# Gate and modulation chunks re-placed beside the second block's attention units, and a barrier crossed with scan work, in a two-block fp32 network kernel

## The reference, cut to what matters

```python
h_l = modulate(xl, norm_mix_g[l], mod_l[0], mod_l[1])        # mod = silu(c) @ ada_w[l] + ada_b[l]
ql, kl, vl, zl, xbcl, dtfl, dtbl, gal, gsl = in_proj_split(h_l @ w_in)
s = jnp.einsum('bqhcd,bkhcd->bchqk', q, k) * (ATT_HEAD_DIM ** -0.5)   # 8 heads, two maps each
p = jax.nn.softmax(s, axis=-1)
a = p[:, 0] - lam * p[:, 1]
o = jnp.einsum('bhqk,bkhe->bqhe', a, v)
att = rmsnorm(o, subln_g) * (1.0 - lam_init)
dt_f = jax.nn.softplus(dtf_raw + dt_bias_f)                  # the scan's time steps, 64 columns of h @ w_in
ssd = ssd_output(...)                                        # conv, two-way chunked scan, norm
merge = (sigmoid(ga) * (att @ w_attn_o) + sigmoid(gs) * ssd) @ w_out
```

## Time and profile before

| | |
|---|---|
| three runs, median (lowest to highest) | 2977.1 us (2976.78 to 2983.97) |
| the profiled execution, its own time | 2984.38 us |
| its span, first to last instruction | 2982.6 us |
| PE busy | 2920.2 us (98%) |
| PEld busy | 2391.0 us (80%) |
| DVE busy | 1452.4 us (49%) |
| ACT busy | 814.4 us (27%) |
| POOL busy | 1019.8 us (34%) |
| mean granted TensorE clock | 0.995 |

### The profile page before, as it was taken

One profiled execution on the slowest core, in us unless ns is written; L12 is line 12 of the kernel. 1 busy time (PEld: TensorE's weight loads), 2 busy tenths in 40 slices (PEclk: granted clock), 3 DMA queues, 4 the chain that ended last, 5 costly groups with the idle time before them and its releaser, 6 DMA issues.

```text
span 2982.6 us, 40515 instructions
## 1 busy us (share of the span) xinstructions
PE 2920.2 (98%) x16088; PEld 2391.0 (80%) x16088; DVE 1452.4 (49%) x2765; ACT 814.4 (27%) x1778; POOL 1019.8 (34%) x876
## 2 busy tenths in 40 slices
PE   8999999999999999999999999999999999999999
PEld 7777899998855558888888888888876766678998
DVE  1243377713265638787753442343247555541651
ACT  1022222201033326766610220111013355540210
POOL 0000333674500125565643244443330112210786
PEclk9999999999999899999999999999999999999999
DMA  7456344442255133222232122222330332234443
GB/s 261 146 208 254 127 156 166 159 170 85 99 212 212 43 128 114 101 112 96 89 129 87 71 96 85 85 85 85 113 113 29 128 113 103 102 121 148 149 170 114
DMA packets 68977, 377.63 MB, mean 127 GB/s; under 512 B 6378, under 2 KB 24874, under 8 KB 26304
## 3 DMA queue, kind: packets, MB, share of 16 engines
q1 hardware_dynamic: 49120, 334.60, 30.9%
q10 hardware_dynamic: 18704, 36.90, 3.7%
q0 software_dynamic: 976, 3.63, 0.3%
HBM read 366.50 MB, written 4.42 MB: 124 GB/s over the span
## 4 chain that ended last, share of the span: by engine, by line
PE 61%; DVE 7%; ACT 2%; PEld 1%; issue 1%; POOL 0%; PEldq 0%; POOLq 0%; ACTq 0%; DVEq 0%
PE PB L501 12%; PE PB L629 9%; PE PA L501 7%; PE PB L1513 6%; PE PS L501 6%; PE PB L381 5%; PE PB L1187 2%; PE PB L1486 2%; PE PB L425 2%; PE PA L1573 1%; PE PA L1609 1%; PE PA L1592 1%; DVE work L2905 1%; ACT work L1984 1%; PE PB L1527 1%; DVE small L2704 1%
## 5 line engine op out<-in xcount | busy, mean ns | idle before, releaser
L536 POOL TENSOR_TENSOR sums<-ring 128x512 f32<-128x512 f32 x115 | 151.2, 1315 | 603.3 <-PE PA L501 246.9
L501 PE MATMUL PB<-work,sums 128*128 128x128 f32 (+1 forms) x1360 | 230.6, 327 | 0.0
L1513 PE MATMUL PB<-H,ring 128*128 128x512 f32 (+1 forms) x576 | 228.3, 545 | 0.0
L501 PEld LDWEIGHTS PB<-work,sums 128*128 128x128 f32 x1360 | 207.1, 191 | 17.5
L501 PE MATMUL PA<-work,sums 128*128 128x128 f32 (+1 forms) x1280 | 208.9, 318 | 0.0
L734 DVE TENSOR_TENSOR work<-PA,work 128x128 f32<-128x128 f32 (+1 forms) x53 | 18.9, 356 | 379.8 <-ACT work L718 379.8
L501 PEld LDWEIGHTS PA<-work,sums 128*128 128x128 f32 x1280 | 187.5, 191 | 13.5
L3204 POOL TENSOR_TENSOR work<-work 128x256 f32<-128x256 f32 x96 | 59.7, 642 | 386.3 <-ACT work L2072 327.1
L1513 PEld LDWEIGHTS PB<-H,ring 128*128 128x128 f32 x576 | 108.7, 191 | 95.7 <-issue 91.4
L734 DVE TENSOR_TENSOR work<-PB,work 128x256 f32<-128x256 f32 (+1 forms) x34 | 13.0, 381 | 320.9 <-ACT work L718 320.9
L541 POOL TENSOR_TENSOR sums<-ring,sums 128x512 f32<-128x512 f32 x115 | 151.6, 1318 | 9.0
(11 more groups left out here) (441 smaller groups left out, 6144.1 us busy)
## 6 DMA issues: line engine op xcount, KB each, us to landing
ring<-stream SPq DMA_DIRECT2D x314, 1024.0 KB, 4.8
sums<-cs_rows ACTq DMA_DIRECT2D x16, 1024.0 KB, 4.6
sums<-cs_rows ACTq DMA_DIRECT2D x16, 512.0 KB, 3.9
work<-work ACTq DMA_DIRECT2D x16, 256.0 KB, 4.4
work<-scratch POOLq DMA_DIRECT2D x1, 2560.0 KB, 13.5
mrg_kept<-work ACTq DMA_DIRECT2D x1, 2048.0 KB, 10.7
work<-mrg_kept ACTq DMA_DIRECT2D x1, 2048.0 KB, 9.7
X<-xT SPq DMA_DIRECT2D x2, 512.0 KB, 5.7
```

The costliest lines, as they stand in the source:

```text
L501: mm = pe.matmul(fast_bank(side, bank)[:, col:col + width], weight(k), right(4 * part + k), start=first and opens and k == 0, stop=last an ...
L536: nc.gpsimd.tensor_tensor(su[:, 0], a21, a22, ALU.add).then_inc(sem("w_summed"), 1)
L1513: mm = pe.matmul(PB[:, pair, t, 0:Tc], ring[:, c % SLOTS, k, t * P:(t + 1) * P], H[:, k, 0:Tc], start=(k == 0), stop=(k == KT - 1))
```

## The change

Four things, with no work added or removed. First, the gate chunks 1 to 3 of layer 0 move from units 12, 20, 28 to 8, 20, 31, and the 24 modulation chunks from units 1 to 24 to units 1 to 30 without 5, 8, 9, 14, 20 and 21. Second, in layer 1 the gate chunks, which stood whole beside units 1, 6 and 11, go by halves: units 1 and 4, 7 and 10, 13 and 16. Third, the last gate chunk's second half is split into four rows of weights each and put into the tail behind the last scores (steps 31 to 33, and 16 and 17 in layer 1). DVE and ACT copy out that last chunk behind their loops. Fourth, at the barrier PE does `project(0, (0,))` between its count and its wait; the time-step product is cut in two, of which one half stands behind the wait and the other behind head 0's sum and `project(0, (1,))`.

```diff
+ADA_BESIDE = [u for u in range(1, 31) if u not in (5, 8, 9, 14, 20, 21)]
+GA_PIECES = [
+    {8: ([(1, 0, 0, KT)], [(1, 1, 0, KT)]), 20: ([(2, 0, 0, KT)], [(2, 1, 0, KT)]), 31: ([(3, 0, 0, KT)], []),
+     32: ([], [(3, 1, 0, 4)]), 33: ([], [(3, 1, 4, KT)])},
+    {1: ([(1, 0, 0, KT)], []), 4: ([(1, 1, 0, KT)], []), 7: ([(2, 0, 0, KT)], []), 10: ([(2, 1, 0, KT)], []),
+     13: ([(3, 0, 0, KT)], []), 16: ([], [(3, 1, 0, 4)]), 17: ([], [(3, 1, 4, KT)])}]
...
-    units, gated = (32, (12, 20, 28)) if la == 0 else (16, (1, 6, 11))
+    units, gated = (32, (8, 20, 31)) if la == 0 else (16, (4, 10, 15))
...
-            + ([(f"ada{la + 1}", u - 1)] if la == 0 and 1 <= u <= ADA_CHUNKS else []) for u in range(units)]
+            + ([(f"ada{la + 1}", ADA_BESIDE.index(u))] if la == 0 and u in ADA_BESIDE else []) for u in range(units)]
...
             eng.drain().then_inc(stage_end, 1)
+            if meanwhile:
+                meanwhile()
             eng.wait_ge(stage_end, 4 * barriers[who])
...
                     if u < len(us):
                         scores2(u)
-                        beside(attention_fill(la)[u], T, 0)
+                        beside(modulation, T, 0)
+                    for piece in ahead:
+                        ga_piece(*piece)
                     if 2 <= u <= len(us) + 1:
                         turn2(u - 2)
-                    if u < len(us):
-                        beside(attention_fill(la)[u], T, 1)
+                    for piece in behind:
+                        ga_piece(*piece)
+                    beside(modulation, T, 1)
                     if u >= 3:
                         values2(u - 3)
                 held.finish(ada_second)
-                bar()
...
+                pe.wait_ge(sem("w_exp"), LAYER["w_exp"] * la + 2 * len(us))
+                bar(lambda: project(0, (0,)))
+                dt_product((0, 1))
                 for h in range(8):
...
-                    project(0, (h,))
+                    project(0, (h + 1,) if h < 7 else ())
+                    if h == 0:
+                        dt_product((2, 3)).then_inc(sem("dt_sum"), 1)
```

More of the change, by code:

```diff
@@ L80 @@
 HALF_AT = [i for i in range(A_UNITS) if i % 8 not in (2, 7)]
+ADA_BESIDE = [u for u in range(1, 31) if u not in (5, 8, 9, 14, 20, 21)]
[4 more added lines that the diff above has]
+     13: ([(3, 0, 0, KT)], []), 16: ([], [(3, 1, 0, 4)]), 17: ([], [(3, 1, 4, KT)])}]
+assert len(ADA_BESIDE) == ADA_CHUNKS
 assert 3 * len(ADA_AT) == ADA_CHUNKS and len(HALF_AT) == 2 * 3 * D // CHUNK
@@ L309, in program, with barrier @@
         barriers = {}
-        def barrier(eng, who):
+        def barrier(eng, who, meanwhile=None):
             barriers[who] = barriers.get(who, 0) + 1
             eng.drain().then_inc(stage_end, 1)
+            if meanwhile:
+                meanwhile()
             eng.wait_ge(stage_end, 4 * barriers[who])
@@ L1077, in _, with bar @@
         def _(pe):
-            def bar():
-                barrier(pe, "pe")
+            def bar(meanwhile=None):
+                barrier(pe, "pe", meanwhile)
             pe.wait_ge(sem("consts"), 1)
@@ L1461, in values2, with ga_piece @@
                     mm.then_inc(sem("w_out"), 1)
+                def ga_piece(j, t, k0, k1):
+                    c, (pair, before) = CHUNKS[f"ga{la}"][j], GROUPS[f"ga{la}"][j]
+                    if t == 0 and k0 == 0:
+                        take_chunk(pe, c, 0, 0)
+                        take_banks(pe, (pair, before), 0, 0)
+                    for k in range(k0, k1):
+                        mm = pe.matmul(PB[:, pair, t, 0:T], ring[:, c % SLOTS, k, t * P:(t + 1) * P],
+                                       H[:, k, 0:T], start=(k == 0), stop=(k == KT - 1))
+                    if t == 1 and k1 == KT:
+                        mm.then_inc(chunk_done, 1)
                 for u in range(len(us) + 3):
+                    modulation = [x for x in attention_fill(la)[u] if x[0].startswith("ada")] if u < len(us) else []
+                    ahead, behind = GA_PIECES[la].get(u, ((), ()))
                     if u < len(us):
                         scores2(u)
-                        beside(attention_fill(la)[u], T, 0)
+                        beside(modulation, T, 0)
+                    for piece in ahead:
+                        ga_piece(*piece)
                     if 2 <= u <= len(us) + 1:
                         turn2(u - 2)
-                    if u < len(us):
-                        beside(attention_fill(la)[u], T, 1)
+                    for piece in behind:
+                        ga_piece(*piece)
+                    beside(modulation, T, 1)
                     if u >= 3:
@@ L1631, in scan_group, with dt_product @@
                     project_z(g, z_tiles[4])
[L1634 to L1638, removed]
+                def dt_product(tiles):
+                    for t in tiles:
+                        for k in range(KT):
+                            mm = pe.matmul(PS[:, 0, 64 * t:64 * t + 64], H[:, k, t * P:(t + 1) * P],
+                                           wdt[:, la, k, :], start=(k == 0), stop=(k == KT - 1))
+                    return mm
+                pe.wait_ge(sem("w_exp"), LAYER["w_exp"] * la + 2 * len(us))
+                bar(lambda: project(0, (0,)))
+                dt_product((0, 1))
                 for h in range(8):
@@ L2000, in _ @@
                         exps2(u)
+                    if u < len(us) - 1:
                         beside(attention_fill(la)[u], ga_out)
+                    if u == len(us) + 2:
+                        beside(attention_fill(la)[-1], ga_out)
                     if u >= 3:
```

## The result

The changed kernel takes 2984.94 us (median of 20 runs, 2983.8 to 2986.23), the kernel before 2976.9 us (20 runs beside it, 2975.14 to 2984.93). The ratio is 1.002, with a 95% interval of 1.0014 to 1.0026: within the 0.3% that counts as no change, inside the forecast range (0.6 us under its upper end), and 5.4 us above the forecast 2979.5. The medians lie 8.0 us apart. The profiled execution after took 2984.13 us, against 2984.38 before.

A forecast was written before the change was run, and what follows sets the result against it. PE, busy 98% of the span, was taken to bound the kernel, with DVE the limiter behind layer 0's time-step product. Terms -4.2 - 1.5 + 2.7 - 3.2 + 1.3 = -4.9 took 2984.4 to 2979.5 us, range 2971 to 2985.5.

The forecast's parts named there:

- Layer 1 behind the barrier: Layer 1 after the attention: time steps 3.7 us later, less 2.3 of DVE's slack, +1.3 us at the last taps.
- layer 0's units: Layer 0's attention: PE's waits fall from 8.3 to 4.1 us as chunks are re-placed, -4.2 us.
- layer 0 behind the attention: Layer 0, last product with the values to second `attn_o` chunk: 70.3 us against 67.6, +2.7 us.
- DVE's slack: Layer 1 behind the barrier: DVE waited 0.75 and 1.59 us for roots, so 2.3 us of delay costs nothing.
- the clock in the tail: Last units of layer 0's attention: gate pieces keep PE busy and its clock at 1.00, -1.5 us.
- at 14 DVE is still ahead from the gate chunk at 8: Layer 0's attention, units 5 and 14 without a chunk: the 0.65 us wait is counted only once.
- the fill does nothing: Rival, both attentions: waits only move to other units, -4.2 and -3.2 are gone, 2986.9 us; chance 0.08.
- the same count: Layer 1's attention: waits of 0.5 at four third units, 1.5 at start, 1.7 at tail; 5.2 against 8.4, -3.2 us.
- the first rival: All runs of before have the low clock, their scatter is from elsewhere; -4.9 applies to the median, 2972 us; chance 0.17.
- PE binds: Rival, behind the barrier: PE sets the pace, not DVE, so clock and waits are won: -18.7, 2965.7 us; chance 0.05.
- the low clock stays through the barrier: Rival, layer 0: PE still falls to half clock in the tail, time steps come later, 2994 us; chance 0.07.
- DVE's 39.3 us: Layer 0 behind the barrier: DVE's first taps come 39.3 us after the time-step product, as before.

The follow-up runs named there:

- Experiment 3: The changed kernel with its new barrier and split product in one layer only, the old ones in the other: layer 0 alone 2979.58 us, layer 1 alone 2975.52 us.
- `whole_product`: The changed kernel with the time-step product in one piece behind the barrier's wait, `project(0, (0,))` still in the wait: 2979.0 us, ratio 1.0003.
- `fill_only`: The changed kernel with the old barrier and time-step product, so only the re-placed gate and modulation chunks remain: 2971.46 us, ratio 0.9977 to the kernel before.
- `barrier_layer1`: The changed kernel with its new barrier and split product in layer 1 alone, the old ones in layer 0: 2975.52 us, ratio 0.9989.
- `barrier_only`: The kernel before with only the new barrier: `project` in the barrier's wait, the time-step product in two halves: 2990.98 us, ratio 1.0045.
- `barrier_layer0`: The changed kernel with its new barrier and split product in layer 0 alone, the old ones in layer 1: 2979.58 us, ratio 0.9998.

## Why the prediction was right, and where it was not

The mechanism held: DVE's list behind the barrier sets the end, and what stands ahead of the time-step product is paid for. The range held by 0.6 us, and that was in part luck: against the median of before the loss is 8.0 us where 2.4 was forecast (2979.5 against 2977.1). Layer 1 behind the barrier came out 3.8 us worse than forecast, layer 0's units with their clock 2.9 worse, and layer 0 behind the attention 2.1 better, which hid part of the two.

*Layer 1 behind the barrier, forecast +1.3, measured +5.1.* This is the step that failed most. The sum "3.60 + 1.84 + 0.5 + 3.60 + 1.84 = 11.3 us" took a quarter of the product for each half: the whole product is 7.36, a half 3.68, as the layer 0 paragraph has it. With that the forecast's own sum is 15.1 us, 7.5 later than before, and +5.2 at the last taps. The time steps come 14.9 us after the last product with the values, 7.1 us later than before's 0.40 + 7.36; less the 2.3 of DVE's slack that is 4.8. The slack was read rightly: the wait of 0.75 and of 1.59 for roots is gone or 0.19 (2318.20 us in DVE's timeline after). Experiment 3 shows the price by itself, 4.1 us by the medians.

*Layer 0's units, forecast -4.2; with the clock in the tail, -1.5, measured -2.8 in all.* The clock held, as said (1.00 from 960 us to the product's end). What failed is "at 14 DVE is still ahead from the gate chunk at 8", and the assumption that units 9 and 21, behind a gate chunk, need no chunk of their own: behind each of the four units without one PE waits 0.53 to 0.69. Waits had moved, so the rival "the fill does nothing" was more than half right for layer 0. In layer 1 the same count (0.5 for each third unit, 1.5, 1.7) gave -3.2, and -3.5 came.

*Layer 0 behind the attention, forecast +2.7, measured +0.6.* The time steps came at 15.3 us (forecast 15.4), PE waited 6.12 us (forecast 8 to 9), and the clock cost 1.48 us there (forecast 1.64). The rule of the Trainium skill, "TensorE: Matmul & The Clock Gate", section "Why this matters for your kernels", that an idle stretch costs the clock, agrees with this wait, and with the one of 3.97 us in `whole_product`. It does not cover every case here: the clock also fell behind the 1.72 us in layer 1, and in before's tail, where no single wait is above 1.20, and it stayed at 1.00 behind the 1.71 us at 2277.08. The 2 us that are missing are DVE's: its first taps ended 37.3 us after the product, not 39.3 (last section).

With the measured terms the forecast's own sum is -2.8 + 0.6 - 3.5 + 5.1 = -0.6, and 2984.4 - 0.6 = 2983.8 us; the profiled run took 2984.1.

*The runs of before.* The inference that those near 2977 ran the tail at full clock and those near 2984 did not is borne out by the mean granted clock of every run before: in the first set the 17 runs at 2975.5 to 2977.4 us have 0.997 to 0.999, the 7 at 2983.6 to 2985.6 have 0.994 or 0.995, with nothing between. So the first rival, that all of them have the low clock, is false. In the second set it is 16 and 13. The changed kernel's 20 runs do not split in this way (all have 0.996), nor the 11 of `fill_only` and the 12 of `barrier_layer1`, which have before's barrier in layer 0: the re-placed chunks do hold the clock in the tail. The 5 runs of `barrier_only`, without them, do not split either, too few to say that the new barrier alone would hold it. A run of before that loses it (2984) takes as long as the changed kernel, and only against the others is the change a loss of 8 us.

*The other rivals.* "PE binds" is refuted by the wait of 6.12 us, "the low clock stays through the barrier" by the window with 1.00 (its terms, +15.4 - 1.3 + 1.5, come to 2995 us, not 2994).

What stays open is why before's tail loses the clock in some runs and not in others; `barrier_only` has the same 1.20 us wait in its tail, and its one profiled run kept the clock at 1.00.

## What to carry to other kernels

Where another engine's long list hangs on a small product, that product comes first behind, or inside, a barrier: work put ahead of it costs up to its full length (3.6 us in each layer for the first `project` here; of the second, layer 1 paid 1.9, since DVE had slack), even if it hides the barrier's 0.4 us. Before a stall is filled, ask which engine's next list starts last; the filler goes behind what starts it. And filler that is split finely (a quarter chunk in two of three units) took the waits of the third unit and of the start too, where halves in one of three left 0.53 each.

## What the runs showed of the hardware

*DVE was slower beside POOL.* DVE's 2 us in layer 0 come from here. DVE's time-step chain before, then POOL beside it:

```profile
1005.02 0.29 DVE L2750 TENSOR_SCALAR work<-work 128x256 f32<-128x256 f32 x1
1005.35 1.01 DVE L2752 TENSOR_SCALAR work<-work 128x256 f32<-128x256 f32 x1
...
1009.10 0.43 DVE L2757 TENSOR_TENSOR work<-work 128x256 f32<-128x256 f32 x1
1009.56 1.16 DVE L2758 TENSOR_TENSOR work<-work 128x256 f32<-128x256 f32 x1
```

```profile
1005.09 1.12 POOL L3174 TENSOR_TENSOR work<-work 128x512 f32<-128x512 f32 x1 [13.75 <-PE PA L1644]
1009.40 1.04 POOL L3174 TENSOR_TENSOR work<-work 128x512 f32<-128x512 f32 x1 [3.19 <-PE PA L1644]
```

The same kind of instruction takes 0.29 us alone and 1.01 beside a square of POOL, another 0.43 and 1.16. After the change the squares fall elsewhere in DVE's list, and the lengths change with them: L2786, which is L2749 before with 0.29, takes 0.68 beside a square, and L2789, the one of 1.01 (L2752 before), takes 0.29 without one.

```profile
1003.12 0.68 DVE L2786 TENSOR_SCALAR work<-work 128x256 f32<-128x256 f32 x1 [0.48 <-ACT work L2048]
...
1004.16 0.29 DVE L2789 TENSOR_SCALAR work<-work 128x256 f32<-128x256 f32 x1
```

```profile
1002.61 1.04 POOL L3211 TENSOR_TENSOR work<-work 128x512 f32<-128x512 f32 x1 [6.83 <-PE PA L1675]
```

The eleven instructions of the chain are 1.06 us shorter (1008.46 - 1001.75 = 6.71 us to the first head, before 7.77), and four instructions of the heads that took 0.80 and three times 0.99 take 0.75, 0.77 less. Together that is the 1.8 us by which DVE's first taps end sooner after its first instruction (37.1 us, before 38.9). I had taken DVE's 39.3 us as fixed. That the squares are the cause is read from the overlap in time; no run moves a square by itself.

*The low clock did not last equally long.* PE is busy for all 13.71 us of before's time-step product, and the granted clock stays at 0.50, 1.2 GHz, to its end. Behind the new wait, in contrast, it is back to 0.72 on the mean of 1040 to 1045 us and to 1.00 in the next 5 us, and the whole loss is 1.48 us. A half clock thus cost 8 us in one place and 1.5 in the other; why it ended sooner there no run shows.

*The price of one wait varied.* PE waits 3.2 us in the scan's last group in every trace. The 16 matmuls behind it, 3.62 us at full clock, took from 5.10 us (`whole_product`) to 6.43 (`barrier_layer0`), with code that no edit touched. The 1.64 us on which the forecast put its price for the clock was one value between 1.5 and 2.8.
